# A two-layer trunk with a mixture of experts: slot tables in two parts, a third late expert, and fewer idle products

## What is computed

```python
def hierarchical_moe(t, wg, bg, we, be, w1, w3, w2):
    g_logit = t @ wg + bg
    g_sel = argmax(g_logit)                      # one of 4 groups
    g_w = softmax(g_logit)[g_sel]
    e_logit = (t @ we + be) of that group        # 8 experts in a group
    top_p, top_i = top_k(softmax(e_logit), 2)
    top_w = top_p / sum(top_p) * g_w
    for e in range(32):
        hidden = silu(t @ w1[e]) * (t @ w3[e])
        y += c[:, e] * (hidden @ w2[e])          # c: top_w where e was chosen, else 0
    return y

# per layer:  x = x + gate_mix * mixer(norm(x));  x = x + gate_moe * hierarchical_moe(norm(x))
# at the end: rmsnorm(x, norm_final)
```

## Time and profile before

| | us |
|---|---|
| median of three runs | 1040.34 |
| lowest and highest | 1038.54, 1044.13 |
| the profiled execution | 1042.62 |
| its span, first to last instruction | 1040.9 |
| PE busy | 965.9 (93%) |
| VectorE busy | 361.2 (35%) |
| ScalarE busy | 248.6 (24%) |
| GpSimd busy | 213.4 (21%) |
| DMA | 315.9 MB, 303 GB/s on average |

### The profile page before, as it was taken

How to read it: one execution, slowest core, us unless ns; L and a number is a source line. 1 busy time by engine, 2 the same in 40 slices (tenths; PEclk the granted TensorE clock), 3 DMA queues, 4 the chain that set the end, 5 groups by cost and what they waited for, 6 DMA issues and landing times.

```text
span 1040.9 us, 17790 instructions
## 1 busy us (share of the span) xinstructions
PE 965.9 (93%) x6151; PEld 612.3 (59%) x6152; DVE 361.2 (35%) x839; ACT 248.6 (24%) x538; POOL 213.4 (21%) x306
## 2 busy tenths in 40 slices
PE   5999999998998899998989899999998999998886
PEld 3444458555886555555555384878875555555552
DVE  4159494564346211110011271145434212221124
ACT  5110002445234122221221250033233111111112
POOL 1008300110001343332331100000002333332310
PEclk9999999999999899998998999999999999999999
DMA  9985545999715699999999899273647998999996
GB/s 357 312 267 172 194 133 214 320 343 380 313 40 208 240 393 406 406 405 407 407 406 407 322 310 328 82 265 108 222 157 242 399 400 301 407 405 404 403 405 248
DMA packets 129081, 315.90 MB, mean 303 GB/s; under 512 B 28891, under 2 KB 59891, under 8 KB 128996
## 3 DMA queue, kind: packets, MB, share of 16 engines
q1 hardware_dynamic: 113200, 295.93, 76.4%
q0 software_dynamic: 10800, 12.72, 3.6%
q10 hardware_dynamic: 4996, 6.09, 1.6%
HBM read 315.07 MB, written 22.31 MB: 324 GB/s over the span
## 4 chain that ended last, share of the span: by engine, by line
PE 75%; DMA 12%; DVE 5%; issue 3%; ACT 2%; SPq 1%; ACTq 0%; POOL 0%; POOLq 0%; DVEq 0%
PE ps L1137 18%; PE ps L941 16%; DMA ring<-in_moe_w 10%; PE ps L993 8%; PE ps L1163 8%; PE ps L951 5%; PE ps L895 3%; PE ps L1109 3%; PE ps L1147 1%; PE ps L1291 1%; SPq L709 1%; DMA pair_out<-RH,sidx_all 1%; DMA RAB<-pair_out 1%; PE ps L929 1%; PE ps L1236 1%
## 5 line engine op out<-in xcount | busy, mean ns | idle before, releaser
L1137 PE MATMUL ps<-ring,RT 128*64 128x256 f32 x2128 | 260.4, 398 | 27.0 <-DMA ring<-in_moe_w 24.2
L1137 PEld LDWEIGHTS ps<-ring,RT 128*64 128x64 f32 x2128 | 164.4, 143 | 97.7 <-issue 24.1
L941 PE MATMUL ps<-RT,ring 128*128 128x512 f32 (+1 forms) x544 | 182.0, 493 | 0.5 <-DVE RT L2309 0.5
L941 PEld LDWEIGHTS ps<-RT,ring 128*128 128x128 f32 x544 | 102.2, 190 | 76.5 <-issue 69.8
L2196 DVE TENSOR_TENSOR RT<-RT,ps 64x256 f32<-64x256 f32 x64 | 27.1, 423 | 270.1 <-ACT RT L1724 149.3
L1163 PE MATMUL ps<-ring,RT 128*64 128x512 f32 x424 | 100.4, 593 | 1.4 <-DVE RT L2202 1.0
L1724 ACT ACTIVATE RT<-ps 64x256 f32<-64x256 f32 x64 | 24.1, 377 | 257.5 <-PE ps L1137 236.3
L2351 DVE SCALAR_TENSOR_TENSOR RAB<-RM,chan,RAB 128x512 f32<-128x512 f32 x120 | 79.7, 748 | 0.0
L2600 POOL DMA_INDIRECT pair_out<-RH,sidx_all x62 | 63.1, 1018 | 55.5 <-POOL sidx_all L2597 51.0
L2576 POOL DMA_INDIRECT RH<-hrow,idx x7 | 8.1, 1156 | 307.5 <-DVE idx L2148 306.0
L2588 POOL DMA_INDIRECT RH<-hrow,sidx_all x56 | 59.2, 1057 | 49.4 <-issue 29.9
(11 more groups left out here) (282 smaller groups left out, 1000.6 us busy)
## 6 DMA issues: line engine op xcount, KB each, us to landing
ring<-in_moe_w SPq DMA_DIRECT2D x358, 512.0 KB
ring<-in_w_mod SPq DMA_DIRECT2D x96, 512.0 KB
ring<-in_odd_w_in SPq DMA_DIRECT2D x24, 512.0 KB
ring<-in_even_w_in SPq DMA_DIRECT2D x20, 512.0 KB
ring<-in_even_w_out SPq DMA_DIRECT2D x8, 512.0 KB
RAB<-in_moe_w SPq DMA_DIRECT2D x8, 512.0 KB, 7.8
RAB<-pair_out SPq DMA_DIRECT2D x8, 512.0 KB, 5.9
ring<-in_odd_w_out SPq DMA_DIRECT2D x8, 512.0 KB
```

Source lines behind the costliest of these rows:

```text
L941: mm = pe.matmul(bank, w[:, c, P * ft:P * (ft + 1)], moving[:, c, :], start=(c == 0), stop=(c == NCH - 1))
L1137: mm = pe.matmul(bank[CAP * k:CAP * (k + 1), 0:BLK], xt(c), w[k][:, BLK * c:BLK * (c + 1)], start=(c == 0), stop=(c == NCH - 1))
```

## The change

Five things are done in one edit.

1. **Slots in two parts.** `slot_rows(l, 1)` now makes only the scatter column of block 0 and both columns of block 1. A new job `("slots", l, 2)`, placed in bank 6, makes blocks 2 and up. On PE it stands behind the first up projection `U(0, 0)`; on VectorE its one-hot tables come after `extra_i`, and its copy to `idx` (`last_slots`) comes after the first hidden rows. `at_slot` has seven buffers instead of two, and the wait for a free one is gone. SP waits for the new job ahead of `in_spare(5)`. GpSimd waits for `all_slots` only for an expert with a third block.
2. **Two choices for several tiles at once.** With more than one tile `two_choices` works on all of them in shared instructions.
3. **Expert 29 is late too.** `LATE` has three experts, each with its own place for its result (`late_rows`). The one-hot tables are transposed for one tile at a time, tile 1 after step 0 of the last group and tile 0 inside step 1, behind its up projection. Expert 29's product for tile 1 stands ahead of the last down projection. One more zero scatter per layer. In layer 0 three late scatters follow the read-back, without the copy of their indices, and VectorE waits for the first of them before it writes the next normalised tile.
4. **Idle products in the last group**: two ahead of each of the last two up projections.
5. **Idle products elsewhere**: five new ones between `slot_rows(0, 1)` and layer 0's first transposes, and six instead of ten at the odd layer's entry.

```diff
@@ psum_plan
     add(("slots", 0, 1), "dve")
+    add(("slots", 0, 2), "dve", bank=SLOTS_BANK)
...
+    add(("slots", 1, 2), "dve", bank=SLOTS_BANK)
@@
-LATE = (EXPERTS - 2, EXPERTS - 1)
+LATE = (EXPERTS - 3, EXPERTS - 2, EXPERTS - 1)
@@ SP, experts
                 sp.wait_ge(routed, l + 1)
                 if l == 1:
                     sp.wait_ge(first_full, 1)
+                full(sp, "slots", l, 2)
                 in_spare(5)
@@ PE, slot_rows
-                for b in range(n_blocks):
+                for b in range(2) if part == 1 else range(2, n_blocks):
                     pe.wait_ge(slot_hot, before + b + 2)
...
-                    if b < n_blocks - 2:
-                        mm.then_inc(slot_used, 1)
@@ PE, step
                     Hd(i, q - 1)
+                    if isinstance(i, int) and i == LAST_GROUP and q >= 2:
+                        pe.wait_ge(x_y_ready, pe.snap(extras))
+                        for _ in range(2):
+                            pe.matmul(ps[:, 7, 0:BLK], ident, const[:, 0:BLK], start=True, stop=True)
                     U(i, q)
                     if isinstance(i, int) and (i, q) == (LAST_GROUP, 1):
-                        pe.wait_ge(late_ready, l + 1)
+                        late_slots(1, LATE_TILES[1])
+                        pe.wait_ge(late_ready, 2 * l + 2)
@@ PE, late_results
+                    late_added(banks, 1, 0)
+                    Dn(LAST_GROUP, PER_LOOP - 1)
+                    used(LAST_GROUP, PER_LOOP - 1, (2,))
+                    late_added(banks, 1, 1)
+                    late_added(banks, 0, 0)
+                    late_added(banks, 0, 1)
+                    late_added(banks, 1, 2)
+                    first_choices(banks, 1)
+                    late_added(banks, 0, 2)
+                    first_choices(banks, 0)
@@ PE, experts
                 if l == 0:
-                    emptied(0)
+                    emptied(0, 1)
                     T(0, 0, start=True)
-                emptied(2)
+                emptied(2, 1)
                 U(0, 0, start=(l == 0))
+                slot_rows(l, 2)
                 emptied(1)
                 T(0, 1, start=(l == 0))
@@ PE, layer 0
             slot_rows(0, 1)
+            warm(("slots", 0, 2), 5)
             experts(0)
@@ PE, odd layer
-            warm(("xT", LATENT, 0), 10)
+            warm(("xT", LATENT, 0), 6)
@@ VectorE, two_choices (several tiles)
+                    for t in range(ts.start, ts.stop):
+                        step(dve.max(best[:, t, :], masked[:, t, :]), wait=False)
+                    step.sync()
+                    for out, k in ((in_two, 1), (cand, 0)):
+                        step(dve.tensor_tensor(out[:, ts, :], masked[:, ts, :], best[:, ts, k:k + 1].broadcast_to([P, n, EXPERTS]),
+                                               ALU.is_ge), wait=False)
+                    step.sync()
+                    step(dve.tensor_tensor(in_two[:, ts, :], in_two[:, ts, :], place, ALU.mult))
+                    step(dve.tensor_tensor(cand[:, ts, :], cand[:, ts, :], in_two[:, ts, :], ALU.add))
...
@@ VectorE, route
-                for j in range(2, n_blocks + 1):
-                    hot(j)
+                hot(2)
...
                 dve.tensor_copy(extra_i[0:1, l, :], words[0:1, :]).then_inc(extra_ready, 1)
+                for j in range(3, n_blocks + 1):
+                    hot(j)
@@ VectorE, experts
                 hidden(0, 0)
+                last_slots(l)
@@ VectorE, layer 0
             late_pair(0)
+            dve.wait_ge(late_scattered[0], 16)
             for t in (1, 0):
                 normed_tile(2, t)
@@ GpSimd, last group
-                    if q + 1 < PER_LOOP:
+                    if q < 2:
                         scatter(LAST_GROUP, q - 1)
...
-                    for q in (PER_LOOP - 2, PER_LOOP - 1):
-                        scatter(LAST_GROUP, q)
+                    for e in range(len(LATE)):
+                        late_scatter(e)
```

210 lines of the change are left out of this document (132 added, 78 removed).

## The result

The changed kernel is slower: 1043.47 us median (11 executions, 1041.7 to 1049.9) against 1040.07 us for the kernel before beside it (11 executions), ratio 1.0043, interval 1.0029 to 1.0058, so 3.0 to 6.0 us. The forecast was 1036.7 us with a range that ended at 1043.0.

A forecast was written before the change was run, and what follows sets the result against it. Expert stages were taken as bound by weight DMA, ending a fixed amount of bytes after the ring's refill starts. Entries -0.9 and -2.1, layer 0's tail with odd entry -1.2, layer 1's tail +0.6: -3.6, so 1036.7 us; range 1033.3 to 1043.0.

The forecast's parts named there:

- What bounds the stages: Expert stages: DMA of weights bounds them; PE time saved before the ring's refill comes off the stage end one for one.
- `two_choices`: Layer 0's entry: shared instructions gain 1.6 us, but everything up to the first gather moves by only -1.0.
- Layer 0's entry, up to U(0,0): Fewer slot groups in front start the first up projection at 339.4 us, 2.8 us earlier; the whole entry was put at -0.9.
- PE then waits some 0.3 us for VectorE to drain them: Layer 0's entry, behind the six moved slot groups: PE waits only some 0.3 us; in layer 1, 0.1.
- -0.9 for D: Layer 1's entry: first up projection 3.67 us at full clock, not 5.36, then 0.6 for moved groups and 0.1 for the drain.
- -1.2 for the earlier start: Layer 1's entry: the first up projection starts 1.2 us earlier, part of -2.1 for that entry.
- The slower rival: Layer 0's entry: the clock falls ahead of the ten idle records, +2.8 there, 1043.5 us in all; chance 0.12.
- SP's new wait: Layer 0's entry: holds the sixth spare slot's load and later ring loads, 2.6 us of DMA, taken by a 6 us dry stretch.
- Layer 0's tail and the odd entry: Layer 0's end and layer 1's beginning: earlier read-back and fewer idle products, -1.2 us together, ends -2.6 and +0.2.
- the idle products in the last group bring nothing: Layer 0's tail: they keep the clock, but the next weights are waited for again, so no gain.
- my -0.6: Both tails with the odd entry: -1.2 and +0.6 us.
- Layer 1's tail: From the last down projection on: 8.6 us instead of 8.3, one piece moved ahead adding 0.3; +0.6 us on the last bank.

The follow-up runs named there:

- e1: The kernel of a1 with 64 increments of an unused semaphore at the start of TensorE's program; ratio 1.0002 to the kernel before.
- c1: The changed kernel with six idle products put ahead of PE's wait for bank 6, all waits and the register load kept; ratio 1.0041 to the kernel before.
- d4: The kernel before with the batch of two_choices over four tiles alone; ratio 0.9984.
- b2: The changed kernel with the extra_ready wait and the counts' load moved behind the first up projection, the bank 6 wait left; ratio 1.0014 to the kernel before.
- a2: The kernel before with the entry parts alone: the batch of two_choices and the split slots with five idle products; ratio 1.0043.
- c3: The changed kernel without the four idle products in the last group of experts; ratio 1.0069 to the kernel before.
- c4: The changed kernel with ten idle products in place of six at the odd layer's entry; ratio 1.0040 to the kernel before.
- d1: The changed kernel with 64 register moves at the start of TensorE's program, which seem not to be in the program; ratio 1.0058 to the kernel before.
- d3: The changed kernel with 256 register moves at the start of TensorE's program, which seem not to be in the program; ratio 1.0047 to the kernel before.
- a4: The kernel before, unchanged, profiled a second time; the profiled execution took 1043.5 us.
- b4: The kernel before, unchanged, profiled a third time; the profiled execution took 1041.99 us.
- a1: The changed kernel with the extra_ready wait and counts' load behind the first up projection, bank 6 awaited only before its first down projection; ratio 0.9992 to the kernel before.
- a3: The kernel before with the tail parts alone: expert 29 late, idle products in the last group, six at the odd layer's entry; ratio 1.0000.
- d2: The kernel of a1 with 64 register moves at the start of TensorE's program, which seem not to be in the program; ratio 0.9978 to the kernel before.
- b1: The changed kernel with only the wait for bank 6 moved, to ahead of the first down projection that writes it; ratio 0.9985 to the kernel before.

## Why the prediction was wrong

- **What bounds the stages**: right. B and E are 212.1 to 212.8 and 213.1 to 213.9 us in all but two profiles (e1's and c1's, told above), whatever the entry was.
- **`two_choices`**: right. The next logits step is at 326.93 in after against 327.87, the first gather at 334.44 against 335.08; d4 gives 1.7 us (0.6 to 2.8) where I had no more than 1.0 for this part. The gather is 0.3 us behind the 334.1 of the sum: it waits for the stored rows.
- **Layer 0's entry, up to U(0,0)**: the mechanism is right. The sum had two values: 339.4 if the clock holds (339.19 in after; six of thirteen profiles), and, as the forecast itself, 335.5 + 4.0 + 0.75 + 0.7 = 340.95 with a clock that falls and comes back during the idle records (340.36 to 340.82 in the five where it did). The six late groups took 1.5 us, not 2.6: they need not be in step with VectorE there.
- **"PE then waits some 0.3 us for VectorE to drain them"**: this is the step that failed, at both entries (0.1 in layer 1). The drain itself was sized well in layer 0, 0.2 us behind T(0,1). In layer 1 it is 0.5, since it comes behind VectorE's part of the hidden rows. But I had asked only when VectorE is done, and not what stands behind the wait in PE's own list, nor that PE's list runs ahead of its products and that a wait ends this: in b2, with nothing left behind the wait, T(0,2) still starts 0.8 to 0.9 us after VectorE is done. In before the load of the counts and the branches ran under U(0,0); behind the new wait they are in the open: 1.95 and 2.14 us in place of 0.3 and 0.1.
- **The clock behind it**: not in the sum. Behind that idle time U(0,1) takes 4.6 to 5.4 us in layer 1, in place of 3.67. In layer 1 the two make D 12.75 to 13.16 us in all six profiles of the split with its waits (after, a2, c3, c4, d1, d3), against 9.57 in before's mean: +3.3, where my terms gave -0.9 for D and -1.2 for the earlier start. The -0.9 rested on one profile: in a4 and b4 U(0,0) of layer 1 had full clock without the change (D 8.86 and 9.35), so there it was not to be had. c1 puts some 1.5 us of it on the clock.
- **The slower rival** (the clock falls ahead of the ten idle records) had a chance of 0.12 and happened in two of thirteen profiles with the split, a2 and d3. Its steps fit a2: idle records 4.63 us (I had 4.4), transposes 1.06 (1.1). U(0,0) then had full clock, which I had not expected, but A came out 4.2 us over before's mean in a2, d3 and c3 (370.0, 369.9, 369.4 against 365.6), not 2.8, by the instructions that came late (1.65 to 2.11) and the 2.0 us ahead of T(0,2).
- **SP's new wait**: 2.2 us in after, and 6.5 and 7.8 in a1 and a2, where the late instructions hold the slots back. I had bounded it by the dry stretch of DMA, and that holds: a1 has A at 364.40 with SP held for 6.5 us.
- **Layer 0's tail and the odd entry**: the mechanisms are there. After's VectorE starts at 590.45 (forecast 590.7) and the odd projection at 603.76 against 605.51. With the earlier start of U(0,0) in layer 1, C is 2.9 us down, where -1.2 and -1.15 were forecast. That the idle products in the last group bring nothing does not fit c3's profile, where the last projection fell to half clock without them and C is 0.7 us longer. The medians (a3) put all of it, with layer 1's tail, between -1.5 and +1.6 us; my -0.6 lies inside.
- **Layer 1's tail**: 0.5 us more from the last U to the end than in the two profiles of before that had full clock there (23.4 against 22.9 and 22.6), forecast 0.6. The sum's list of rows leaves out the second 1.12 (1029.62 us); its 8.3 has it. What it did not have: in a4, a2 and d4 the old tail's last projection ran at half clock and F is 23.9 to 24.0, so over the five profiles with that tail (mean 23.5) F is no shorter than with the change.
- **Not in the sum at all**: the instructions that come late, 1.65 to 2.19 us in the executions that have them.

The stretches summed: A is the mean of the two kinds, (365.2 + 369.8) / 2 - 365.6 = +1.9; D +3.3; C -2.9; F +0.3: +2.6 us. The comparison says 3.0 to 6.0. The half-and-half weight for A is that of the six profiles; only two of after's own eleven executions are above 1045 us, and with so few of the upper kind A would be near +0.4 and the sum near +1. So the stretches do not account for all of the loss. The direction is in line with a3: C's gain is smaller in the medians than in the profiles.

Of all kernels run, two are under the kernel before with their whole interval: d2 (0.9978, 0.9961 to 0.9995), which as far as can be seen is a1's program, and the batch alone, d4 (0.9984, 0.9973 to 0.9994). a1 itself had 0.9992 (0.9974 to 1.0009), so the change with its waits moved lies between 4 us less and 1 us more, and is not clearly better than the batch by itself. No run kept the split and took its five idle products away, so what these cost or bring in layer 0 is not known.

## What to carry to other kernels

When a wait is added to an engine's list, read what stands behind it in that list up to the next product, register loads and branches among it: they were free only as long as the list ran ahead. Put such a wait at its first real user, and loads of registers ahead of it. When a single profile shows no difference and the median does, profile again and cut the span at fixed instructions: two kinds of executions show in one stretch.

## What the runs showed of the hardware

- PE's next product starts 0.76 and 0.89 us after the end of the VectorE instruction that its list waits for (b2, layers 0 and 1).
- A register load with its branches behind such a wait adds 0.7 us to PE's idle time in layer 1 (2.14 in after, 1.41 in b2). Without that wait it shows there as 0 to 0.45 us (a4, b4, b1), and as 0.88 in layer 0 of b1.
- 2 us of idle PE (after, layer 1) were followed by a projection partly at 1.2 GHz, PEclk 0.50: 5.04 us in place of 3.67. Twelve unused records in that idle time kept it at 2.4 GHz (c1).
- A packet of PE's instructions can come late when weights are on the way, and idle time of 1.65 to 2.19 us goes with it; PE goes on 2.0 to 2.7 us behind the packet. The Trainium skill, "Runtime: NRT & Kernel Launch", section "Instruction fetch mechanics", says that instructions are fetched over DMA in blocks of 16 KiB, 256 instructions, and that the cost of crossing into a new block is mostly hidden. The size agrees with the page of the profile (56 packets, 0.92 MB, 16.4 KB each). "Mostly hidden" does not hold here: seven of thirteen profiles with the split show the idle time, and with the blocks shifted (e1) idle time stands at a new place. By that sentence it would cost the change next to nothing; measured, it goes with A at 369.4 to 370.0 us in place of 364.5 to 366.1 where the split has its waits as in the change, and of this difference the idle time itself is 1.65 to 2.11, the slow idle records another 1.4 to 2.2.
